# Two half transfers for every expert weight block in a two-layer hybrid trunk

## The chip, the cores and the metric

One core of one Trainium2 chip runs the whole program. The metric is the device time of one execution in microseconds (us), from the first to the last instruction and what lies around it; the median of the runs counts.

## What is computed

Two layers of an encoder trunk on 256 tokens of width 1024, all in fp32. Each layer has a token mixer and a channel mixer, both with norms and conditioning. The channel mixer of layer 0 is a dense SwiGLU; that of layer 1 sends each token to 2 of 8 experts. The change touches the experts alone:

```python
def swiglu(u, wg, wu, wd):
    return (jax.nn.silu(u @ wg) * (u @ wu)) @ wd

def moe_swiglu(h, w_router, b_router, w_gate_e, w_up_e, w_down_e):
    ...
    logits = (t @ w_router).astype(jnp.float32) + b_router.astype(jnp.float32)
    top_val, top_idx = lax.top_k(logits, TOP_K)
    gates = jax.nn.softmax(top_val, axis=-1)
    ...
    def expert_block(args):
        xblk, e = args
        return swiglu(xblk, w_gate_e[e], w_up_e[e], w_down_e[e])
    yb = lax.map(expert_block, (xb, blk_e)).reshape(p, d)
    y = jnp.zeros((n, d), h.dtype).at[tok_sorted].add(yb[dest] * g_sorted[:, None].astype(h.dtype))
```

The hidden width of an expert is 3584, so gate, up and down of one expert hold 3 x 14 = 42 MiB in fp32, and the eight experts 336 MiB. The other weights (about 120 blocks of up to 1 MiB) come before them through half of the same buffers.

## The kernel before

Each engine runs a program of its own, written out by hand; semaphores tie them together.

**Blocks and slots.** The weights of an expert are cut into 14 stages of 256 hidden columns. A stage has one block for gate and one for up (`[128, 8, 256]`: for each of 8 slices k of the input, 256 columns) and one for down (`[128, 2, 1024]`: for each of 2 halves f of the hidden columns, 1024 outputs). Each block is 1 MiB, 8 KB in each of 128 partitions, and lies in memory as 128 rows of 8 KB. Blocks are used in the order gate, up, then the down block of the stage before (`expert_uses`, lines 112 to 119). They go round 14 slots (`ring_e`, line 405): seven are the ring of the earlier weights (`ring` in the views), seven lie in the `arena`. In an expert 42 blocks go through, three rounds of the slots.

**SP** issues the transfers. `expert_use(i, e)` (lines 646 to 650) issues block i of expert e, which raises the semaphore `landed_e` of its slot by 16. Ahead of it SP waits until TensorE has done with the block that was in the slot (`last_use`, line 652: `gu_full` for gate and up, `down_done` for down). Three blocks of expert 0 are issued early; the loop from line 664 does all others, each one 14 blocks ahead of its use.

**TensorE** loops over the experts from line 1125. It reads the expert's number of tokens and branches to one of six versions of the code (`variants`, lines 545 to 554), for 32, 64, 128, 160, 192 or 256 tokens, each a tile of up to 128 tokens, or two. A version gathers the expert's tokens (lines 1140 to 1153), and then goes through the tiles of the 14 stages: `gate_up` of tile i, `turn` (a transpose of the activations) of tile i - 1, `down` of tile i - 2 (lines 1207 to 1217). Lines 1220 to 1228 spread the result back over the tokens. With fewer than 128 tokens in a tile `gate_up` uses line 1176: for each k, all of gate's and up's products, side by side in the array. With 128 it uses line 1182: all k for gate, then all k for up. `down` is line 1203, f outermost.

The waits for the weights are in `weights` (lines 1159 to 1162): `gate_up` waits for both blocks before its first product, `down` for its block before it waits for the activations (`at_ready`):

```python
def weights(kind, s):
    i = expert_at[kind, s]
    pe.wait_ge(landed_e[i % SLOTS_E], e * (16 * USES // SLOTS_E) + 16 * (i // SLOTS_E + 1))
    return ring_e[i % SLOTS_E]
```

**ScalarE and VectorE** take the gate products through silu and multiply with up (`act_ready`), and copy what `turn` made (`at_ready`). They don't look at `landed_e`.

In this input the experts run one behind the other as follows (widths of the version; times are from the views): experts 0 and 1 with 32, expert 2 with 128, expert 3 with 64, expert 4 with 160 (tiles of 128 and 32), expert 5 with 32, expert 6 with 192 (tiles of 128 and 64), expert 7 with 64.

Of the kernel before, what the change touches and what calls it, by code (L numbers as in the profile page):

```python
# [27 lines left out]
KD = D // P  # L28
# [13 lines left out]
SLOTS, SW = 7, 256  # L42
# [3 lines left out]
USES = 3 * STAGES  # L46
# [3 lines left out]
SLOTS_E = 2 * SLOTS  # L50
# [190 lines left out]
def build(nc, ap, out):  # L241
# [4 lines left out]
    expert_at = {u: i for i, u in enumerate(expert_list)}  # L246
# [8 lines left out]
    with ExitStack() as ctx:  # L255
# [6 lines left out]
        def sem(name):  # L262
            return ctx.enter_context(nc.semaphore(name))
# [69 lines left out]
        def cut(user, *dims):  # L333

            n = int(np.prod(dims))
            a = arena[:, top[user]:top[user] + n]
            top[user] += n
            return shaped(a, *dims)
# [66 lines left out]
        ring_e = [ring[:, (n_before + i) % SLOTS, :, :] for i in range(SLOTS)] + [cut("ffn", KD, SW) for _ in range(SLOTS_E - SLOTS)]  # L405
# [40 lines left out]
        wl_in = sem("wl_in")  # L446

        landed = [sem(f"landed{i}") for i in range(SLOTS)]
        landed_e = [sem(f"landed_e{i}") for i in range(SLOTS_E)]
        out_read = sem("out_read")  # L450
        const_set = sem("const_set")
        pj_full = sem("pj_full")
# [69 lines left out]
        def dense_use(kind, s):  # L522
            return 3 * s + KINDS.index(kind)
# [36 lines left out]
        def gate_up_of(m, u):  # L560

            w = SW if m > 32 else P
            if m == P:
                return PG[:, u % 2, 0:w], PG[:, u % 2, w:2 * w], slice(0, P), w
            return PG[0:P // 2, u % 2, 0:w], PG[P // 2:P, u % 2, 0:w], slice(P // 2, P), w
# [13 lines left out]
        def outputs(j, m):  # L581

            if m == P:
                return [(Y[:, 2 * j + h, :], h * 512, 512) for h in range(2)]
            n = P // m
            w = D // n
            return [(Y[i * m:(i + 1) * m, 2 * j + 2 * i // n, 0:w], i * w, w) for i in range(n)]

        def at_unit(e, n, u):


            return e * FT + (FT + (u + 1) * (2 // len(blocks(n))))

        def at_own(e, n, u):

            return e * FT + (u + 1) * (2 // len(blocks(n)))
# [21 lines left out]
        @block.sync  # L618
        def _(sp):
            def last_reader(kind, a, b):  # L620

                if kind == "ada":
                    return tr_full, TR.full(("ada", a, b // 4))
                if kind == "in":
                    return pj_full, PJ.full((IN_ITEM[b], a))
                if kind == "out":
                    return (y_full, 2 + a) if b == D // SW - 1 else (out_read, (D // SW - 1) * a + b + 1)
                return split_lo, dense_use(kind, b) + 1

            at = 0  # L630
            for u, (kind, a, b) in enumerate(uses):
                if u >= SLOTS:
                    sp.wait_ge(*last_reader(*uses[u - SLOTS]))
                n = KD * (b[1] if kind == "in" else SW)
                slot = ring[:, slot_of[u], :, :]
                if n < KD * SW:
                    slot = slot[:, :, 0:n // KD]
                else:
                    slot = slot.rearrange("p k c -> p (k c)")
                src = ap["weights"][0:1, at:at + P * n].rearrange("o (p c) -> p (o c)", p=P)  # L640
                if n < KD * SW:
                    src = src.rearrange("p (k c) -> p k c", k=KD)
                at += P * n
                sp.dma_start(slot, src).then_inc(landed[slot_of[u]], 16)

            def expert_use(i, e):

                slot = ring_e[i % SLOTS_E].rearrange("p k c -> p (k c)")
                src = ap["experts"][bass.ds(e * (USES * P) + i * P, P), :]
                sp.dma_start(slot, src).then_inc(landed_e[i % SLOTS_E], 16)  # L650

            def last_use(i, e):


                kind, s = expert_list[(i - SLOTS_E) % USES]
                return down_done if kind == "down" else gu_full, e * FT + ((FT if i >= SLOTS_E else 0) + 2 * s + 2)


            for i in range(EARLY):
                sp.wait_ge(*last_reader(*uses[n_before - SLOTS + i]))  # L660
                expert_use(i, 0)
            sp.wait_ge(y_full, 3)

            with sp.Fori(0, NE - 1) as e:
                for i in range(EARLY, USES):
                    sp.wait_ge(*last_use(i, e))
                    expert_use(i, e)
                for i in range(EARLY):
                    sp.wait_ge(*last_use(i, e + 1))
                    expert_use(i, e + 1)  # L670
            for i in range(EARLY, USES):
                sp.wait_ge(*last_use(i, NE - 1))
                expert_use(i, NE - 1)
            for b in range(TB):
                sp.wait_ge(out_ready, 2 * (b + 1))
                sp.dma_start(out[0][b * P:(b + 1) * P, :], tok[:, b, :]).then_inc(out_done, 16)
            sp.wait_ge(out_done, 16 * TB)
# [5 lines left out]
        def _(pe):  # L683
# [441 lines left out]
            with pe.Fori(0, NE) as e:  # L1125
                n_tok = pe.value_load(cnt[0:1, bass.ds(e, 1)], min_val=0, max_val=T)

                def expert(n):
# [11 lines left out]
                    for i in range(4):  # L1140
                        bank = take()
                        for j in range(2):
                            k = 2 * i + j
# [13 lines left out]
                    step = 2 // len(blocks(n))  # L1157

                    def weights(kind, s):
                        i = expert_at[kind, s]  # L1160
                        pe.wait_ge(landed_e[i % SLOTS_E], e * (16 * USES // SLOTS_E) + 16 * (i // SLOTS_E + 1))
                        return ring_e[i % SLOTS_E]

                    def gate_up(u, s, j, m):

                        w = [weights("gate", s), weights("up", s)]
                        if u >= 2:
                            pe.wait_ge(act_ready, at_unit(e, n, u - 2))
                        bank = PG[:, u % 2, :]
                        x = mixT[:, :, j * P:j * P + m]  # L1170
                        if m < P:
                            width = gate_up_of(m, u)[3]
                            for k in range(KD):
                                for i in range(P // m):
                                    c = i * width
                                    last = mm(bank[i * m:(i + 1) * m, 0:width], x[:, k, :],  # L1176
                                              w[c // SW][:, k, c % SW:c % SW + width],
                                              start=(k == 0), stop=(k == KD - 1))
                        else:
                            for i in range(2):  # L1180
                                for k in range(KD):
                                    last = mm(bank[:, i * SW:(i + 1) * SW], x[:, k, :], w[i][:, k, :],  # L1182
                                              start=(k == 0), stop=(k == KD - 1))
                        last.then_inc(gu_full, step)
# [12 lines left out]
                    def down(u, s, j, m):  # L1197

                        w = weights("down", s).rearrange("p k c -> p (k c)").rearrange("p (f c) -> p f c", f=2)
                        pe.wait_ge(at_ready, at_own(e, n, u))  # L1200
                        for f in range(2):
                            for o, c, width in outputs(j, m):
                                last = mm(o, actT[:, u % 2, f, 0:m], w[:, f, c:c + width],  # L1203
                                          start=(s == 0 and f == 0), stop=(s == STAGES - 1 and f == 1))
                        last.then_inc(down_done, step)

                    us = units(n)
                    for i in range(len(us) + 2):
                        if i < len(us):
                            gate_up(*us[i])  # L1210
                        if i == 0:
                            for b in range(2):
                                pe.wait_ge(ax_free[b], e * AX_F[b] + (AX_F[b] + 2))
                        if 1 <= i <= len(us):
                            turn(*us[i - 1])
                        if i >= 2:
                            down(*us[i - 2])

                    pe.wait_ge(ye_ready, e * 2 + 2)
                    for i in range(4):  # L1220
                        bank = take()
                        bl = blocks(n)
                        for q in range(2):
                            k = 2 * i + q
# [837 lines left out]
```

## Time and profile before

| what | value |
|---|---|
| median of 3 runs | 2094.73 us |
| lowest and highest of them | 2093.11 us and 7076.81 us |
| the profiled execution, its own time | 2095.57 us |
| its span, first to last instruction | 2093.8 us |
| TensorE's mean granted clock (1 is 2.4 GHz) | 0.883 |
| TensorE busy with products | 1811.4 us, 87% |
| weight queue q1 | 478.02 MB in 71616 packets |
| expert transfers | 336 of 1024.0 KB |

One of the three runs was far off; the other two lie within 2 us. In the views L1176 is line 1176 of the kernel, PE is TensorE's products and PEld its weight loads, "PEldq" and "SPq" are the sequencers of TensorE and SP, and q1 is SP's DMA queue; q8 and q14 carry the program's code. A DMA share of 1.00 means that the packets of all queues took the time of all sixteen DMA engines; a little over 1 is how packets are booked at a window's edges. In this table 1 MB is 10^6 bytes, and a block is 1.0486 MB.

### The profile page before, as it was taken

The numbers are of one execution on the slowest core, as the hardware profiler recorded it, in microseconds if no ns is written. First come the engines' busy times: TensorE is split into PE (matmuls) and PEld (weight loads), VectorE is DVE, ScalarE is ACT, GpSimd is POOL, SyncE is SP. The second block draws the span as 40 slices with busy tenths as digits, with TensorE's granted clock in tenths as the row PEclk, the third lists the DMA queues.
The fourth block names the chain that finished last, engine by engine and source line by source line (L and its number), as shares of the span: only waits on it lengthen the run. The fifth ranks groups of instructions, "written<-read, shape, count | busy, mean of one in ns | idle before, by whom it ended". The sixth has DMA issues, their size and how long they took to land.

```text
span 2093.8 us, 32178 instructions
## 1 busy us (share of the span) xinstructions
PE 1811.4 (87%) x13586; PEld 1349.1 (64%) x13587; DVE 443.5 (21%) x971; ACT 299.3 (14%) x585; POOL 43.1 (2%) x48
## 2 busy tenths in 40 slices
PE   3998979999899897665679979699997689999796
PEld 2776759999776676554467755477665466666453
DVE  1152235555415222111010011110011010000112
ACT  1222133333212211101000000100000010000101
POOL 0010000000001001000000000000000000000000
PEclk7997689999998767878789989799997889999797
DMA  6732357555342135599977759946463974444393
GB/s 235 286 121 80 149 188 286 183 183 189 131 147 110 75 155 223 240 419 402 420 316 288 297 205 417 388 164 240 196 241 159 420 318 181 181 181 181 112 418 139
DMA packets 75639, 484.86 MB, mean 232 GB/s; under 512 B 11872, under 2 KB 16236, under 8 KB 17516
## 3 DMA queue, kind: packets, MB, share of 16 engines
q1 hardware_dynamic: 71616, 478.02, 57.5%
q10 hardware_dynamic: 3756, 3.39, 0.6%
q8 instruction: 155, 2.54, 0.5%
q14 instruction: 112, 0.92, 0.1%
HBM read 480.33 MB, written 1.05 MB: 230 GB/s over the span
## 4 chain that ended last, share of the span: by engine, by line
PE 82%; issue 7%; DMA 5%; DVE 3%; ACTq 1%; ACT 1%; POOL 1%; SPq 0%; DVEq 0%; POOLq 0%
PE PG L1182 14%; PE Y L1203 13%; PE PG L1176 11%; DMA arena<-in_experts 5%; PE Y L796 4%; PE TRB L1193 3%; PE Y L804 3%; PE TRB L736 3%; PE Y L1049 3%; PE PG L760 3%; PE PG L762 3%; PE PG L761 3%; PE PG L1226 2%; PE TRB L1146 1%; PE TRB L1226 1%
## 5 line engine op out<-in xcount | busy, mean ns | idle before, releaser
L1960 DVE COPY arena<-TRB 128x64 f32<-128x64 f32 (+2 forms) x140 | 42.6, 305 | 835.4 <-PE TRB L1193 835.4
L1253 ACT ACTIVATE arena<-PG 128x256 f32<-128x256 f32 (+2 forms) x168 | 57.8, 344 | 1019.8 <-PE PG L1176 513.8
L1176 PE MATMUL PG<-ring,mixT 128*32 128x128 f32 (+1 forms) x2640 | 159.8, 320 | 28.2 <-issue 26.5
L1176 PE MATMUL PG<-arena,mixT 128*32 128x128 f32 (+1 forms) x2288 | 146.2, 336 | 36.3 <-issue 36.3
L1203 PE MATMUL Y<-arena 128*32 128x256 f32 (+2 forms) x896 | 171.6, 489 | 3.4 <-issue 3.4
L1176 PEld LDWEIGHTS PG<-ring,mixT 128*32 128x32 f32 (+1 forms) x2640 | 119.3, 124 | 75.3 <-issue 51.3
L1182 PE MATMUL PG<-ring,mixT 128*128 128x256 f32 x720 | 160.7, 381 | 1.3 <-DVE mixT L1943 1.3
L1176 PEld LDWEIGHTS PG<-arena,mixT 128*32 128x32 f32 (+1 forms) x2288 | 108.6, 131 | 78.5 <-issue 58.5
L1182 PEld LDWEIGHTS PG<-ring,mixT 128*128 128x128 f32 x720 | 135.4, 190 | 29.3 <-issue 11.9
L1182 PE MATMUL PG<-arena,mixT 128*128 128x256 f32 x624 | 139.9, 380 | 0.0
L760 PE MATMUL PG<-h_parts,parts 128*128 128x256 f32 x448 | 126.8, 283 | 10.0 <-DVE parts L1854 10.0
L1182 PEld LDWEIGHTS PG<-arena,mixT 128*128 128x128 f32 x624 | 117.0, 189 | 26.5 <-issue 10.2
L1203 PE MATMUL Y<-ring,arena 128*32 128x256 f32 (+2 forms) x672 | 127.9, 482 | 1.9 <-issue 1.9
L762 PE MATMUL PG<-h_parts,parts 128*128 128x256 f32 x448 | 126.8, 283 | 0.0
L761 PE MATMUL PG<-h_parts,parts 128*128 128x256 f32 x448 | 125.6, 280 | 0.0
L1146 PE MATMUL TRB<-arena,tok 128*128 128x128 f32 (+2 forms) x128 | 32.3, 446 | 89.3 <-issue 89.3
L1203 PEld LDWEIGHTS Y<-arena 128*32 128x32 f32 (+2 forms) x896 | 60.8, 134 | 71.5 <-issue 58.5
L1854 DVE TENSOR_TENSOR parts<-ring,parts 128x2048 fp32r<-128x2048 f32 x42 | 95.9, 2292 | 25.7 <-ACT parts L1253 25.7
L796 PE MATMUL Y<-hT,ring 128*128 128x256 f32 x416 | 95.3, 390 | 0.0
L760 PEld LDWEIGHTS PG<-h_parts,parts 128*128 128x128 f32 x448 | 85.4, 191 | 10.8 <-DVE parts L1854 10.4
L1146 PEld LDWEIGHTS TRB<-arena,tok 128*128 128x128 f32 x128 | 30.0, 330 | 94.0 <-issue 94.0
L1193 PEld LDWEIGHTS TRB<-con,arena 128*128 128x128 f32 (+1 forms) x448 | 62.8, 191 | 42.5 <-issue 40.5
(295 smaller groups left out, 2230.4 us busy)
## 6 DMA issues: line engine op xcount, KB each, us to landing
ring<-in_experts SPq DMA_DIRECT2D x168, 1024.0 KB, 9.1
arena<-in_experts SPq DMA_DIRECT2D x168, 1024.0 KB, 15.5
ring<-in_weights SPq DMA_DIRECT2D x116, 1024.0 KB, 6.3
ring<-in_weights SPq DMA_DIRECT2D x4, 512.0 KB, 4.0
tok<-in_x ACTq DMA_DIRECT2D x1, 1024.0 KB, 13.7
result<-tok SPq DMA_DIRECT2D x2, 512.0 KB, 2.8
ring<-in_weights SPq DMA_DIRECT2D x2, 432.0 KB, 6.2
arena<-in_w_ukv ACTq DMA_DIRECT2D x2, 384.0 KB, 4.2
```

Source lines behind the costliest of these rows:

```text
L736: last = mm(bank[32 * c:32 * c + 32, 0:SW], ccol[:, k, :], ring[:, slot_of[u], k, :], start=(k == 0), stop=(k == KD - 1))
L760: mm(out_, w_hi[w][:, c], x[0], start=first, stop=False, skip_group_check=True)
L761: mm(out_, w_hi[w][:, c], x[1], start=False, stop=False, skip_group_check=True)
L762: return mm(out_, w_lo[w][:, c], x[0], start=False, stop=last, skip_group_check=True)
L796: last = mm(bank_part, ring[:, s, k, c:c + m], hT[:, k, :], start=(k == 0), stop=(k == KD - 1))
L1146: last = mm(bank[:, j * T:j * T + w], tok[:, b, k * P:(k + 1) * P], oh[:, b, 0:w], start=(b == 0), stop=(b == TB - 1))
L1176: last = mm(bank[i * m:(i + 1) * m, 0:width], x[:, k, :], w[c // SW][:, k, c % SW:c % SW + width], start=(k == 0), stop=(k == KD - 1))
L1182: last = mm(bank[:, i * SW:(i + 1) * SW], x[:, k, :], w[i][:, k, :], start=(k == 0), stop=(k == KD - 1))
L1193: last = mm(tr[u % 2][:, f * P:(f + 1) * P], actK[r, u % 2, f * P:(f + 1) * P], ident[r, :], start=True, stop=True)
L1203: last = mm(o, actT[:, u % 2, f, 0:m], w[:, f, c:c + width], start=(s == 0 and f == 0), stop=(s == STAGES - 1 and f == 1))
L1226: last = mm(bank[:, q * T:(q + 1) * T], yeK[0:m, j, k * P:(k + 1) * P], gPT[0:m, j, :], start=(j == 0), stop=(j == len(bl) - 1))
L1854: V.tensor_tensor(w_lo[d % SPLITS], ring[:, slot_of[slot_of_dense(d)], :, :].rearrange("p k c -> p (k c)"), w_hi[d % SPLITS].bitcast(F32), ...
```

## The change

Each slot has two semaphores, `landed_e[slot][0]` and `[1]`. `expert_use` issues two transfers of `[128, 1024]`: the first 4 KB of each partition (slices k = 0 to 3 of gate and up, f = 0 of down), and the second 4 KB. Both are behind the one wait for the slot. On TensorE `weights` no longer waits. `half_landed(kind, s, q)` waits for half q of a block; `gate_up` calls it at k = 0 and k = 4, in a tile narrower than 128 for gate and up together, in a tile of 128 for the one in hand; `down` calls it ahead of each f. Nothing is computed differently.

```diff
-        landed_e = [sem(f"landed_e{i}") for i in range(SLOTS_E)]
+        landed_e = [[sem(f"landed_e{i}_{q}") for q in range(2)] for i in range(SLOTS_E)]
...
                 slot = ring_e[i % SLOTS_E].rearrange("p k c -> p (k c)")
                 src = ap["experts"][bass.ds(e * (USES * P) + i * P, P), :]
-                sp.dma_start(slot, src).then_inc(landed_e[i % SLOTS_E], 16)
+                for q in range(2):
+                    o = slice(q * KD * SW // 2, (q + 1) * KD * SW // 2)
+                    sp.dma_start(slot[:, o], src[:, o]).then_inc(landed_e[i % SLOTS_E][q], 16)
...
                     def weights(kind, s):
+                        return ring_e[expert_at[kind, s] % SLOTS_E]
+
+                    def half_landed(kind, s, q):
                         i = expert_at[kind, s]
-                        pe.wait_ge(landed_e[i % SLOTS_E], e * (16 * USES // SLOTS_E) + 16 * (i // SLOTS_E + 1))
-                        return ring_e[i % SLOTS_E]
+                        pe.wait_ge(landed_e[i % SLOTS_E][q], e * (16 * USES // SLOTS_E) + 16 * (i // SLOTS_E + 1))
...
                             for k in range(KD):
+                                if k % (KD // 2) == 0:
+                                    half_landed("gate", s, k // (KD // 2))
+                                    half_landed("up", s, k // (KD // 2))
                                 for i in range(P // m):
...
                                 for k in range(KD):
+                                    if k % (KD // 2) == 0:
+                                        half_landed(("gate", "up")[i], s, k // (KD // 2))
                                     last = mm(bank[:, i * SW:(i + 1) * SW], x[:, k, :], w[i][:, k, :],
                                               start=(k == 0), stop=(k == KD - 1))
...
                         for f in range(2):
+                            half_landed("down", s, f)
                             for o, c, width in outputs(j, m):
```

On TensorE, this is `gate_up`, `turn` and `down` of one tile of 128 tokens, in the version for two tiles, first before, then after the change. `landed_e2` and `landed_e3` are the semaphores of the slots of gate and up, `landed_e4` that of down; a second number is the half.

```order
L1182 MATMUL PG<-ring,mixT 128x256 [waits act_ready,landed_e3,landed_e2]
L1182 MATMUL PG<-ring,mixT 128x256 x15
L1188 REGISTER_ALU
L1193 MATMUL TRB<-con,arena 128x128 [waits act_ready]
L1193 MATMUL TRB<-con,arena 128x128
L1200 REGISTER_ALU [waits landed_e4]
L1203 MATMUL Y<-ring,arena 128x512 [waits at_ready]
L1203 MATMUL Y<-ring,arena 128x512 x3
```

```order
L1191 MATMUL PG<-ring,mixT 128x256 [waits landed_e2_0,act_ready]
L1191 MATMUL PG<-ring,mixT 128x256 x3
L1191 MATMUL PG<-ring,mixT 128x256 [waits landed_e2_1]
L1191 MATMUL PG<-ring,mixT 128x256 x3
L1191 MATMUL PG<-ring,mixT 128x256 [waits landed_e3_0]
L1191 MATMUL PG<-ring,mixT 128x256 x3
L1191 MATMUL PG<-ring,mixT 128x256 [waits landed_e3_1]
L1191 MATMUL PG<-ring,mixT 128x256 x3
L1197 REGISTER_ALU
L1202 MATMUL TRB<-con,arena 128x128 [waits act_ready]
L1202 MATMUL TRB<-con,arena 128x128
L1209 REGISTER_ALU
L1213 MATMUL Y<-ring,arena 128x512 [waits landed_e4_0,at_ready]
L1213 MATMUL Y<-ring,arena 128x512
L1213 MATMUL Y<-ring,arena 128x512 [waits landed_e4_1]
L1213 MATMUL Y<-ring,arena 128x512
```

No product has moved; the one wait point for the blocks of gate and up has become four, and the one of down two, inside the rows of products.

On SP, this is the issue of three blocks inside the loop over the experts, first before, then after.

```order
L650 ISA [waits down_done]
L650 DMA arena<-in_experts 128x2048
L666 REGISTER_ALU
L650 ISA [waits gu_full]
L650 DMA arena<-in_experts 128x2048
L650 ISA [waits gu_full]
L650 DMA arena<-in_experts 128x2048
```

```order
L668 REGISTER_ALU
L652 ISA [waits gu_full]
L652 DMA ring<-in_experts 128x1024
L652 ISA
L652 DMA ring<-in_experts 128x1024
L652 ISA [waits gu_full]
L652 DMA ring<-in_experts 128x1024
L652 ISA
L652 DMA ring<-in_experts 128x1024
L652 ISA [waits down_done]
L652 DMA arena<-in_experts 128x1024
L652 ISA
```

Each wait for a slot now stands ahead of two transfers instead of one; the order of the blocks is the same.

## Rows read from the trace of the kernel before

**Rows 1.** The page, part 4: the chain that ended last, by engine.

```profile
PE 82%; issue 7%; DMA 5%; DVE 3%; ACTq 1%; ACT 1%; POOL 1%; SPq 0%; DVEq 0%; POOLq 0%
```

**Rows 2.** Stretches of the expert phase: experts 0-1; 5; 2; 3; 4; 7.

```profile
core 0: us, PE busy (x) PEld busy (x) DVE busy (x) ACT busy (x) POOL busy (x), PEclk, DMA share, GB/s
858.80:1036.60 177.80, 114.96 (x2158) 86.73 (x2149) 19.40 (x66) 12.45 (x35) 0.00 (x0) 0.82 1.00 411
1602.60:1670.90 68.30, 45.26 (x964) 33.71 (x956) 6.52 (x25) 4.69 (x14) 0.00 (x0) 0.90 0.99 410
...
1061.00:1222.00 161.00, 158.85 (x650) 119.17 (x649) 13.84 (x36) 8.31 (x19) 0.00 (x0) 0.97 0.75 293
...
1239.00:1331.00 92.00, 90.75 (x653) 53.76 (x654) 12.85 (x36) 7.96 (x19) 0.00 (x0) 0.97 0.88 363
...
1352.00:1575.00 223.00, 220.88 (x1816) 155.16 (x1816) 24.07 (x68) 12.95 (x36) 0.00 (x0) 0.97 0.54 210
...
1975.00:2066.00 91.00, 89.75 (x653) 52.67 (x653) 12.85 (x36) 7.96 (x19) 0.00 (x0) 0.98 0.79 324
```

**Rows 3.** TensorE's waits (total us, times, longest), 858 to 1037; then 1036 to 2070.

```profile
PE PG L1176 <- issue: 41.5, 18, 4.1
...
PE PG L1176 <- issue: 23.9, 10, 4.1
```

**Rows 4.** TensorE in order of time (start, us), two stages and the last of expert 1.

```profile
999.50 3.64 PE L1176 MATMUL PG<-arena,mixT 128*32 128x128 f32 x64 [4.07 <-issue]
...
1006.95 1.96 PE L1176 MATMUL PG<-arena,mixT 128*32 128x128 f32 x64 [1.47 <-issue]
...
1036.72 3.65 PE L1176 MATMUL PG<-arena,mixT 128*32 128x128 f32 x64 [2.57 <-issue]
```

**Rows 5.** DMA, 980 to 1030 us: queue, kind: packets, MB, share; issues and us to landing.

```profile
q1 hardware_dynamic: 2869, 20.90, 100.5%
...
ring<-in_experts SPq DMA_DIRECT2D x12, 1024.0 KB, 25.8
```

**Rows 6.** TensorE's branches (ns min/median/max, first and last start): four under load, two quiet.

```profile
L1125 PEldq COMPARE_BRANCH  x1: 6055/6055/6055, 1046.3 to 1046.3; - x1
...
L551 PEldq COMPARE_BRANCH  x1: 5925/5925/5925, 1222.2 to 1222.2; - x1
...
L1125 PEldq COMPARE_BRANCH  x1: 7177/7177/7177, 1336.6 to 1336.6; - x1
...
L551 PEldq COMPARE_BRANCH  x3: 70/80/6456, 1686.4 to 1686.6; - x3
...
L553 PEldq COMPARE_BRANCH  x1: 3344/3344/3344, 1956.0 to 1956.0; - x1
...
L551 PEldq COMPARE_BRANCH  x3: 82/3894/4897, 1965.1 to 1969.2; - x3
```

**Rows 7.** DMA, 2089 to 2093.8 us: the two result transfers, pieces of 4 KB.

```profile
q1 hardware_dynamic: 288, 1.05, 54.6%
```

**Rows 8.** DMA, 126 to 130.5 us: one weight transfer of 512 KB, pieces of 512 bytes.

```profile
q1 hardware_dynamic: 1040, 0.52, 38.6%
```

**Rows 9.** The chain in order of time (start, us), two stages of expert 3.

```profile
1259.65 3.47 PE PG L1176 x32
...
1265.62 3.47 PE PG L1176 x32
```

**Rows 10.** TensorE's sequencer at the wait for weights (ns min/median/max).

```profile
L1161 PEldq EVENT_SEMAPHORE  x24: 51/51/51, 856.5 to 1982.1; - x24
```

**Rows 11.** TensorE in order of time (start, us), a stage of expert 2.

```profile
1102.35 3.60 PE L1203 MATMUL Y<-arena 128*128 128x512 f32 x8
1105.79 1.46 PE L1182 MATMUL PG<-arena,mixT 128*128 128x256 f32 x6
```

**Rows 12.** SP's transfers to the arena and all landings (min/median/max), 1100 to 1210 us.

```profile
L650 SPq DMA_DIRECT2D arena<-in_experts x16: 332/333/333, 1106.1 to 1204.5; - x16
...
DMA to landing us min/median/max: 4.7/6.7/9.6
```

## The prediction

> **What bounds the kernel now.** I read four things in this order. First the chain that ended last [rows 1]: TensorE carries 82% of it, "issue" 7% and DMA 5%. So the whole is a TensorE kernel, and a change to weight transfers can only act where the chain leaves TensorE.
>
> Then the table of stretches [rows 2]. The experts run from about 858 to 2066 us, and there are two kinds. In the first stretch (experts 0 and 1, few tokens) and the second one (expert 5) the DMA engines are busy at a share of 1.00 and 0.99 while TensorE is busy for 115.0 of 177.8 us and 45.3 of 68.3 us: these wait for weights. In the other four TensorE is busy for over 98% of the time and the DMA share is 0.54 to 0.88 (expert 6, not shown, is like expert 4): there the ring of 14 blocks is full or filling. The waits of L1176 with "issue" as their cause are 41.5 us over 18 times up to 1037 us and 23.9 us over 10 times behind it [rows 3]. Here "issue" is the wait for `landed_e`, which the view doesn't name.
>
> Third, the pace inside a starved expert [rows 4]. The products of two successive stages begin at 999.50 and 1006.95 us: 7.45 us for three blocks, 2.48 us a block. In the window 980 to 1030 us the weight queue's packets take 100.5% of the sixteen engines, and a transfer lands 25.8 us after its issue [rows 5], some ten blocks of 2.48 us: about ten transfers are queued. So the queue is never empty there, and what sets the time is engine time per block, not the wait of one product.
>
> Fourth, what TensorE does between experts. The branches into the next expert's code take from 5.93 to 7.18 us while weights are moving, and 3.34 to 4.90 us while the queue is quiet [rows 6].
>
> **The price of a block in two halves.** A whole block is 128 pieces of 8 KB and 16 semaphore writes, 144 packets; the halves make 256 pieces of 4 KB and 32 writes, 288 packets. In rows 5 the queue moves 20.90 MB (19.93 blocks) in 1.005 x 16 x 50 = 804 us of engine time, 40.3 us a block, or 2.52 us on each of 16 engines. The two result transfers are exactly the new shape, 256 pieces of 4 KB with 32 small ones, though they write to HBM: 0.546 x 16 x 4.8 = 41.9 us [rows 7], 2.62 us a block, 0.10 more. The weight transfer with pieces of 512 bytes took 0.386 x 16 x 4.5 = 27.8 us for half a block [rows 8], 3.47 us a block with 2080 packets. By these two shapes a packet costs (55.6 - 40.3) / (2080 - 144) = 8 ns, and 144 packets more cost 1.14 us of engine time, 0.07 us a block. The bounds of a loss are thus 0.07 near by and 0.95 (the 512-byte row) far off; a gain is excluded, since no byte goes away. I take 0.08, between the two near rows.
>
> It counts only where DMA decides. By rate times time of rows 2, 411 GB/s over 177.8 us is 70 blocks, and 410 GB/s over 68.3 us is 27. So +5.6 us for experts 0 and 1, and +2.2 us for expert 5.
>
> Experts 3 and 7 could become starved, since a stage takes 5.97 us (1259.65 to 1265.62) [rows 9] and eats three blocks, of which DMA brings 5.97 / 2.48 = 2.4 now and 5.97 / 2.56 = 2.33 later. Over 14 stages that draws 8.4 blocks now and 9.4 later from a stock of 14. They stay TensorE's: nothing.
>
> **What earlier halves give.** In a starved expert each stage may begin when the first half of `up` is there, 1.28 us sooner. That makes TensorE early, but the last half still comes at DMA's pace and the ring still has ten transfers queued, so the next stage is not sooner by it. It counts once where DMA's chain hands over to TensorE: the last stage of expert 1 (3.65 us of products from 1036.72 [rows 4], of which the first half now lies before the second half's landing) and the same place in expert 5. Each gains at most a half's time, 1.28 us, since half of 3.65 is more than that; for both I take -2.6 us. At the far end, the release of a slot to SP comes with the last product as before and gives nothing.
>
> **The added waits.** The two waits for gate and up of a tile become four (one more place in a tile narrower than 128, three more at 128), and the one for down becomes two. They stand in the row of products, so all of TensorE's later products queue behind them, and ScalarE and VectorE behind those. Where the half has landed they are only sequencer work: 51 ns for a semaphore instruction [rows 10]. The L1182 group at 1105.79 follows the down products of 1102.35 + 3.60 = 1105.95 without a gap, though three waits stand before it, as the order above shows [rows 11]. So at 128 tokens they cost nothing, hidden by products of 0.2 us. The narrowest tiles issue fastest; in expert 4 there are 14 of them. Two more semaphore instructions and a register one, at most 0.14 us each, make 0 to 1.9 us; I take 1.0. In starved experts the wait for DMA covers them. If the cover were gone there too (42 tiles), it would be 6 us.
>
> **SP.** Twice the issues: 0.33 us each [rows 12] with 0.1 us of registers, under 0.9 us a block against 2.56. If ten transfers is what the queue holds, ten halves are 12.8 us of work queued instead of 25; a lone transfer needs 4.7 us from issue to landing [rows 12], so the queue still doesn't run dry.
>
> **Code loading.** TensorE's branch instructions wait for code that comes over the same 16 engines. Under load eight of them lie on the chain (two between experts 1 and 2, one behind expert 2, three behind 3, two behind 5), mean 6.45 us; the seven quiet ones have 4.14 [rows 6]; of the eight the first, both extremes and the last are shown, of the seven the extremes. The excess of 2.3 us is time behind queued weights. What of it goes with halves isn't shown by any row: between 0 (if the loader waits behind bytes) and all of it. An engine's share of one transfer is 2.5 us now, close to the excess, and 1.28 us then. I take it that the loader waits for about a transfer's share, and that the excess halves: 8 x 1.15 = -9.2 us. Between experts 0 and 1 it gives nothing, for DMA is the chain there.
>
> The Trainium skill (DMA: Bandwidth & Descriptors, Queues, rings and completion order) says that an engine takes turns between its queues at whole packets of some 9 to 17 descriptors, and one transfer here is nine to each engine. By that rule the sum would be the one I take; by turns at every 8 KB piece, 0.31 us now (2.52 / 8) and half later, it would be -1 us for this term. The trace's excess of 2.3 us is far above one piece, so it leans to the rule.
>
> **Sum.** +5.6 + 2.2 - 2.6 + 1.0 - 9.2 = -3.0 us, on the profiled execution's 2095.57 us: 2092.6. The median of the runs, 2094.73, lies 0.8 us below that execution, so 2092 for the median.
>
> **Rivals.** *Loader unmoved*: branches stay at 6.45 us under load, and what is left is the packet price at experts 0, 1 and 5: +6.2 us, 2101, slower than before. For it: the 16 KB code packets themselves can't be split by the change, and engines may queue by bytes. Against: the excess is so near to one transfer's share. It decides as soon as less than 6.2 / 8 = 0.8 us goes from each branch.
>
> *The waits shrink*: each of the 28 waits of rows 3 becomes 1.28 us shorter: -36 us, 2059. Against it are the DMA share of 1.00 and the strict 7.45 us.
>
> *Half blocks move slowly*: a 4 KB piece of an 8 KB row is read worse than the result's own, up to the 512-byte price: 97 blocks x 0.95 = +92 us, and experts 3 and 7, then starved (5.97 / 3.47 = 1.7 blocks a stage, 18 of a stock of 14), some 10 us more: 2200. It passes 2% from 2.95 us a block on. Against: both near rows. The Trainium skill (DMA: Bandwidth & Descriptors, Rules for kernel authors) wants at least 1 MiB per transfer; its fixed cost of about 2 us per transfer, if paid in turn, would go this way. Rows 5 bear it out only as latency: with ten queued, 2.5 us is all that a block takes.
>
> *The change does nothing that shows*: both terms small, 2095.
>
> **Chances.** Forecast 0.47, loader unmoved 0.36, waits shrink 0.05, slow halves 0.05, nothing 0.07. The low end is the whole excess gone (-18.4) with free waits: 2095.57 - 0.8 + 5.6 + 2.2 - 2.6 - 18.4 = 2082, say 2083. The high end is the loader unmoved, with 0.10 a block (+2), waits at 1.9 (+0.9) and no gain at the hand-over (+2.6): 2107. A measurement of this kernel tells about 2% (42 us) from no change. Beyond it on the fast side only a far stronger form of the shrinking waits lies, 0.01; on the slow side most of slow halves, 0.04; within, 0.95.
>
> **What would show it.** Right: in a starved stretch the queue's share stays at 1.00 and the stage takes 3 x 2.56 = 7.7 us; stages of experts 2, 3, 4, 6 and 7 keep their times; branches under load fall to about 5.3 us; transfers land some 13 us after their issue. Loaded branches above 6.2 us would make the forecast wrong in favour of the first rival, a share below 0.95 or a stage above 8.3 us in favour of slow halves, and a stage below 7.3 us in favour of shrinking waits.

## The result, and the profile after

The changed kernel took 2101.92 us (median of 10 runs, 2099.15 to 2107.13), the kernel before beside it 2097.2 us (median of 10). The ratio of the means, without the one far-off run of the kernel before, is 1.0031, 95% interval 1.0019 to 1.0044: about 6.5 us slower (4.7 us by the medians). A second set, shown below, gave 1.0045 (1.0027 to 1.0062). Both are inside the stated range, but the forecast had the sign wrong; what came is nearest to the rival that was called *loader unmoved*, with its 2101 us.

The profiled execution took 2100.6 us, its span 2098.8 us. The page's chain and weight queue, to be held against [rows 1]:

```profile
q1 hardware_dynamic: 120000, 478.04, 60.3%
...
PE 75%; SPq 8%; issue 7%; DMA 4%; DVE 3%; ACT 1%; ACTq 1%; POOL 1%; DVEq 0%; POOLq 0%
```

The same bytes move in 120000 packets instead of 71616, which is 336 x 144 more, and take 60.3% of the engines' time. "SPq 8%" is new in the chain. I don't read it as a cost by itself: an issue takes up to 2.9 us in the starved stretch and 0.33 us where the queue has room, so SP is held back while the queue is full. The chain is followed through SP there instead of through the transfers and TensorE, whose share falls from 82% to 75%. The DMA engines have a share of 1.01 in the same stretch, so they never wait for SP. A DMA-bound stretch is booked in another place.

The stretches that answer to those of [rows 2] (experts 0-1; 5; 2; 3; 4; 7):

```profile
core 0: us, PE busy (x) PEld busy (x) DVE busy (x) ACT busy (x) POOL busy (x), PEclk, DMA share, GB/s
860.00:1043.20 183.20, 116.59 (x2169) 87.14 (x2158) 19.40 (x66) 12.55 (x35) 0.00 (x0) 0.80 1.01 397
1606.00:1675.40 69.40, 47.93 (x904) 34.67 (x904) 6.41 (x25) 3.21 (x12) 0.00 (x0) 0.83 1.02 401
1064.00:1225.00 161.00, 158.17 (x650) 118.74 (x650) 13.62 (x36) 8.93 (x20) 0.00 (x0) 0.98 0.84 302
1243.00:1337.00 94.00, 90.96 (x651) 54.14 (x652) 12.84 (x36) 7.95 (x19) 0.00 (x0) 0.97 0.89 345
1357.00:1578.00 221.00, 217.71 (x1816) 153.59 (x1816) 24.05 (x68) 12.92 (x36) 0.00 (x0) 0.99 0.61 218
1980.00:2072.00 92.00, 89.83 (x653) 52.84 (x653) 12.84 (x36) 7.95 (x19) 0.00 (x0) 0.99 0.82 321
```

The first two rows are starved as before, with a full DMA share, but the rate has gone from 411 to 397 GB/s and from 410 to 401 GB/s.

TensorE in order of time (start, us) in two starved stages of expert 1, and the last one; this answers to [rows 4]:

```profile
1027.92 3.64 PE L1183 MATMUL PG<-ring,mixT 128*32 128x128 f32 x64 [2.73 <-DMA ring<-in_experts]
...
1035.60 1.08 PE L1183 MATMUL PG<-arena,mixT 128*32 128x128 f32 x32 [1.57 <-DMA arena<-in_experts]
1036.88 1.08 PE L1183 MATMUL PG<-arena,mixT 128*32 128x128 f32 x32 [0.19 <-DMA arena<-in_experts]
...
1043.28 3.21 PE L1183 MATMUL PG<-arena,mixT 128*32 128x128 f32 x64 [3.91 <-DMA arena<-in_experts]
```

Two things can be read here. The stages come 7.68 us apart instead of 7.45. And the halves do what they are for: at 1035.60 TensorE works on the first half, waits, and begins the second at 1036.88, 1.28 us later, as the second half lands. At 1027.92, with the products slower than the transfer, there is no gap. TensorE is early in every stage, and the next stage is not a bit sooner for it.

DMA from 980 to 1030 us, for [rows 5]:

```profile
q1 hardware_dynamic: 5583, 20.33, 101.9%
...
ring<-in_experts SPq DMA_DIRECT2D x15, 512.0 KB, 15.9
```

A half lands 15.9 us after its issue; at 1.28 us each about twelve are queued.

TensorE's branches (ns, min/median/max), for [rows 6], four under load and two quiet:

```profile
L1127 PEldq COMPARE_BRANCH  x1: 6052/6052/6052, 1051.7 to 1051.7; - x1
...
L551 PEldq COMPARE_BRANCH  x1: 6934/6934/6934, 1225.3 to 1225.3; - x1
...
L1127 PEldq COMPARE_BRANCH  x1: 7312/7312/7312, 1343.0 to 1343.0; - x1
...
L551 PEldq COMPARE_BRANCH  x1: 6556/6556/6556, 1691.0 to 1691.0; - x1
...
L553 PEldq COMPARE_BRANCH  x1: 3677/3677/3677, 1960.4 to 1960.4; - x1
...
L551 PEldq COMPARE_BRANCH  x3: 82/4359/4591, 1970.0 to 1974.5; - x3
```

Nothing fell. The eight loaded branches on the chain have a mean of 6.53 us, before 6.45. The spread between executions is as large: in the traces of the experiments below the same eight have 6.42 us in the repeat of the change and 6.43 us in the first experiment, which also has halves, against 6.48 and 6.43 us in the two kernels with whole blocks and ten queued.

The last two stages of expert 3, which the prediction had left out of the sum:

```profile
1312.09 3.62 PE L1183 MATMUL PG<-ring,mixT 128*64 128x256 f32 x32
...
1318.05 3.64 PE L1183 MATMUL PG<-arena,mixT 128*64 128x256 f32 x32
...
1325.49 3.69 PE L1183 MATMUL PG<-arena,mixT 128*64 128x256 f32 x32 [1.30 <-DMA arena<-in_experts]
```

The last gap is 7.44 us, of which 1.30 us are a wait for DMA. A stage of expert 3 took 5.97 us [rows 9], and in the trace of before the last ones are as long:

```profile
1307.23 3.62 PE L1176 MATMUL PG<-ring,mixT 128*64 128x256 f32 x32
...
1313.19 3.64 PE L1176 MATMUL PG<-arena,mixT 128*64 128x256 f32 x32
...
1319.16 3.64 PE L1176 MATMUL PG<-arena,mixT 128*64 128x256 f32 x32
```

The last of these stages was already close to its block there. SP issued the `up` block of stage 13 in the kernel before as follows, and it landed 17.2 us later, at 1318.8 us, 0.4 us ahead of its first use at 1319.16:

```profile
L650 SPq DMA_DIRECT2D arena<-in_experts x1: 333/333/333, 1301.6 to 1301.6; - x1
...
DMA to landing us min/median/max: 17.2/17.2/17.2
```

In expert 7 it landed at 2053.0 us and was used from 2053.94.

### The profile page after: what moved, and what is told of

Its sections match the earlier page's. It is cut to its first block, busy times and chain, and to the rows that moved or that the text cites. A ratio compares the mean times of both kernels' runs of the same rounds, so it can differ in the third digit from the quotient of the medians.

```text
span 2098.8 us, 33330 instructions
## 1 busy us (share of the span) xinstructions
PE 1809.9 (86%) x13586; PEld 1347.0 (64%) x13587; DVE 443.4 (21%) x971; ACT 299.0 (14%) x585; POOL 43.0 (2%) x48
## 3 DMA queue, kind: packets, MB, share of 16 engines
q1 hardware_dynamic: 120000, 478.04, 60.3%
## 4 chain that ended last, share of the span: by engine, by line
PE 75%; SPq 8%; issue 7%; DMA 4%; DVE 3%; ACT 1%; ACTq 1%; POOL 1%; DVEq 0%; POOLq 0%
PE PG L1191 14%; PE Y L1213 11%; PE PG L1183 8%; SPq L652 8%; PE Y L798 4%; DMA arena<-in_experts 4%; PE Y L806 3%; PE TRB L1202 3%; PE Y L1051 3%; PE PG L762 3%; PE PG L764 3%; PE PG L763 3%; PE TRB L738 2%; PE PG L1236 2%; PE TRB L1148 1%
## 5 line engine op out<-in xcount | busy, mean ns | idle before, releaser
L1213 PEld LDWEIGHTS Y<-arena 128*32 128x32 f32 (+2 forms) x896 | 60.3, 134 | 67.2 <-issue 54.5
```

Of the source, the lines that this page charges most:

```text
L1213: last = mm(o, actT[:, u % 2, f, 0:m], w[:, f, c:c + width], start=(s == 0 and f == 0), stop=(s == STAGES - 1 and f == 1))
```

## The experiments

The theory after the result ("starved" is a stretch in which TensorE waits for blocks, the "hand-over" its end, where TensorE sets the pace again, and the "loader" whatever fetches TensorE's code): (a) a packet costs a fixed time, which counts in starved stretches; (b) experts 3 and 7 have become starved at their ends; (c) TensorE's hand-over from the last starved block gains once per starved expert chain; (d) met waits are free; (e) the loader's excess depends neither on pieces nor on the queue. All ratios are to the kernel before in the same set.

**Halves without the new waits.** Against the kernel before:

```diff
-                sp.dma_start(slot, src).then_inc(landed_e[i % SLOTS_E], 16)
+                for q in range(2):
+                    o = slice(q * KD * SW // 2, (q + 1) * KD * SW // 2)
+                    sp.dma_start(slot[:, o], src[:, o]).then_inc(landed_e[i % SLOTS_E], 16)
...
-  pe.wait_ge(landed_e[i % SLOTS_E], e * (16 * USES // SLOTS_E) + 16 * (i // SLOTS_E + 1))
+  pe.wait_ge(landed_e[i % SLOTS_E], e * (32 * USES // SLOTS_E) + 32 * (i // SLOTS_E + 1))
```

> Two transfers of 512 KB per block, both raising one semaphore by 16, and TensorE waits as in the kernel before, once for the whole block (32 per use). Theory (the price is engine time per block, 0.08 us, at about 97 starved blocks, and experts 3 and 7 turn starved at their end): without the hand-over gain the time is 2 to 5 us above the changed kernel, so +8 to +12 us against the kernel before; a starved stage takes 7.68 us. Rival (the added waits inside the products cost the time): this kernel has none of them and is within 2 us of the kernel before.

Measured: 1.0064 (1.0047 to 1.008), 2108.03 against 2094.36 us, +13.4 us by the ratio. The interval, +9.8 to +16.8 us, reaches into the theory's +8 to +12, and the loss is 1.4 to 2 times that of the full change (+9.4 and +6.5 us); the rival is out. TensorE at the end of expert 3:

```profile
1310.68 3.62 PE L1178 MATMUL PG<-ring,mixT 128*64 128x256 f32 x32
...
1317.32 3.69 PE L1178 MATMUL PG<-arena,mixT 128*64 128x256 f32 x32 [0.51 <-issue]
...
1324.99 3.69 PE L1178 MATMUL PG<-arena,mixT 128*64 128x256 f32 x32 [1.48 <-issue]
```

6.64 and 7.67 us instead of 5.97 and 5.97: 2.4 us lost by the starts of products, and as much in expert 7. The `up` block of stage 13 landed at 1324.9 us here, just before the 1324.99. With the waits per half the same place loses 1.5 us in expert 3 and 1.1 us in expert 7 (1.4 and 0.8 us in the repeat below), since the last stage may begin at the first half. From the same trace, the time from the first product of expert 0 to the last stage of expert 1 is 5.7 us longer than before, and that from expert 5's first product to its last stage 2.1 us.

**The new waits without the halves.** Against the changed kernel:

```diff
-                for q in range(2):
-                    o = slice(q * KD * SW // 2, (q + 1) * KD * SW // 2)
-                    sp.dma_start(slot[:, o], src[:, o]).then_inc(landed_e[i % SLOTS_E][q], 16)
+                sp.dma_start(slot, src).then_inc(landed_e[i % SLOTS_E][0], 16)
...
-                        pe.wait_ge(landed_e[i % SLOTS_E][q], e * (16 * USES // SLOTS_E) + 16 * (i // SLOTS_E + 1))
+                        pe.wait_ge(landed_e[i % SLOTS_E][0], e * (16 * USES // SLOTS_E) + 16 * (i // SLOTS_E + 1))
```

> One transfer of 1 MB per block as before, but TensorE waits at all the places of the changed kernel, for the same semaphore each time. Theory: met waits are hidden, 0 to +2 us against the kernel before, and the first products of up in the 128-wide tiles may start before up has landed, which gives nothing. Rival (waits carry the loss): +5 to +7 us, and stages of experts 2, 4 and 6 get longer by 0.1 us or more each.

Measured: 0.9994 (0.9985 to 1.0002), at most +0.4 us. No cost of the waits shows. In expert 4, the one with the narrow tiles that the prediction gave 1.0 us, TensorE reads

```profile
1392.93 1.96 PE L1181 MATMUL PG<-ring,mixT 128*32 128x128 f32 x64
...
1407.64 0.62 PE L1181 MATMUL PG<-arena,mixT 128*32 128x128 f32 x13
```

and a stage is 14.71 us, as from 1394.93 to 1409.64 us in the kernel before. Even mid-row waits at a product spacing of 0.03 us (64 products in 1.96 us) are hidden.

**Pieces of 4 KB in one transfer.** Source and destination written as three dimensions:

```diff
-  sp.dma_start(slot, src).then_inc(landed_e[i % SLOTS_E], 16)
+  sp.dma_start(slot.rearrange("p (h c) -> p h c", h=2),
+               src.rearrange("p (h c) -> p h c", h=2)).then_inc(landed_e[i % SLOTS_E], 16)
```

> One transfer per block, one semaphore, waits as before, but source and destination are written as 128 x 2 x 1024, so that a block should move in 256 pieces of 4 KB with 16 semaphore writes. Theory (a fixed 8 to 9 ns per packet): 128 packets more a block instead of 144, so nine tenths of e1's loss, +7 to +10 us, starved stage 7.66 us. Rival (the second transfer costs, by its issue or its semaphore writes): within 2 us of the kernel before. If the pieces stay 8 KB nothing changes and the run only repeats the kernel before.

Measured: 0.9994 (0.9984 to 1.0004). It tells nothing of pieces: the page has 71616 packets on q1 as before, so the two dimensions were joined again. It is a repeat of the kernel before, and shows that this comparison is good to 0.1%. So it doesn't tell whether the smaller pieces or the second transfer and its semaphore writes cost; the packets' own records do, under the next run.

**Quarters.** As the first experiment with four transfers and 64 per block.

> Four transfers of 256 KB per block (pieces of 2 KB) on one semaphore, waits as in the kernel before. Theory (a fixed 8 to 9 ns per packet): 576 packets a block instead of 144, three times the added packets of e1, 0.24 us a block: starved stage 8.2 us, and three times e1's loss, about +39 us. Rival (a fixed price per transfer, or none below some size): twice e1's loss or less, +27 us at most. The branches under load: about 6.5 us again if the loader doesn't wait behind a transfer's share, near 5 us if it does.

Measured: 1.0205 (1.0191 to 1.022), +43 us, 3.2 times the +13.4 us of halves. A starved stage:

```profile
1031.72 3.64 PE L1178 MATMUL PG<-ring,mixT 128*32 128x128 f32 x64 [3.06 <-issue]
...
1039.86 2.86 PE L1178 MATMUL PG<-ring,mixT 128*32 128x128 f32 x64 [2.15 <-issue]
```

8.14 us. Single stages scatter, so I take several of expert 1 for the price: 7.44 us a stage in the kernel before (five stages, 999.50 to 1036.72), 7.66 us in the first experiment (five, 1004.06 to 1042.34) and 8.11 us here (four, 1015.52 to 1047.94). For each added packet that is 0.21 / 3 x 16 / 144 = 7.8 ns with halves and 0.66 / 3 x 16 / 432 = 8.1 ns with quarters: about 8 ns, and straight.

Halves and quarters add transfers in the same proportion as packets (one and three a block), so these times alone would fit a price per transfer as well. The packets' own records decide. From 970 to 1030 us a piece of 8 KB is booked at 314 ns on average, one of 4 KB at 165 ns and one of 2 KB at 88 ns, so two pieces take 11 to 16 ns more than one of twice the size; a semaphore write is booked at 9 ns, and the 16 added with halves are 0.15 us of the 1.2 us of engine time that a block in halves costs. The share of the engines stays above 1.00, so nothing is lost between transfers. It is 1.005, 1.019 and 1.046 for whole blocks, halves and quarters from 980 to 1030 us, more than packets at a window's edges explain: booked times overlap a little, so the price of 8 ns is taken from the stages and not from the records.

The eight loaded branches have a mean of 6.2 us, 96% of the 6.45 us before. But they didn't all stay. The first ones behind experts 1, 3 and 5 took 5.03, 4.69 and 5.24 us instead of 6.05, 6.10 and 6.28; the other five took 6.5 to 7.4 us, 0.35 us more than before on average. What makes the first ones shorter is open.

**A queue of three, and of two.** Whole blocks; SP waits for the landing of an earlier block (its loop over the experts written out, so that waits are on constants):

```diff
+                o = i - 3
+                if o >= 0:
+                    sp.wait_ge(landed_e[o % SLOTS_E], e * (16 * USES // SLOTS_E) + 16 * (o // SLOTS_E + 1))
...
-            with sp.Fori(0, NE - 1) as e:
+            for e in range(NE - 1):
```

> Whole blocks, but SP issues block i only when block i - 3 has landed, so that three transfers are queued at most instead of ten (the loop over the experts is written out on SP so that waits are on constants). Theory A (the loader's excess under load of 2.3 us does not depend on what is queued): branches stay at 6.5 us, the stage at 7.45 us, and the time within -2 to +3 us of the kernel before. Theory B (the loader waits behind queued bytes): branches fall to 5.5 us or less and the time by 6 to 15 us.

> As e6_queue_of_three with two transfers at most. A lone transfer takes 4.7 us to land, of which 2.3 us are not its own bytes, so two queued ones just don't cover it on every engine: starved stages of 7.5 to 8.5 us, the time +5 to +40 us. Theory A: branches under load still 6 to 6.5 us; theory B: 5 us or less, since engines run dry between blocks.

Measured: three 0.9998 (0.9984 to 1.0013), two 1.0158 (1.0131 to 1.0185), +33 us. With three queued a transfer lands 7.4 us after its issue instead of 25.8 [rows 5], and the branches stay:

```profile
ring<-in_experts SPq DMA_DIRECT2D x10, 1024.0 KB, 7.4
...
L1131 PEldq COMPARE_BRANCH  x1: 5752/5752/5752, 1051.9 to 1051.9; - x1
...
L551 PEldq COMPARE_BRANCH  x1: 6036/6036/6036, 1224.0 to 1224.0; - x1
...
L1131 PEldq COMPARE_BRANCH  x1: 7117/7117/7117, 1338.7 to 1338.7; - x1
...
L551 PEldq COMPARE_BRANCH  x3: 70/80/6296, 1691.6 to 1691.9; - x3
```

Mean of the eight: 6.46 us. Theory B is out: whether three transfers are queued or ten doesn't matter to the loader. With two queued, when the share of the DMA engines falls to 0.95, the first branches behind experts 1, 2, 3 and 5 take 4.7, 3.7, 4.3 and 4.6 us, and the second at each of these places still takes 6 us and more.

The pace with three queued isn't quite that of ten in the profiled execution, which at 2101.44 us was the slowest of its twelve: from 980 to 1030 us it moved 406 GB/s against 420, and seven stages of expert 1 came 7.7 us apart on average, not the expected 7.45. The time of all twelve shows no loss.

**Halves for the last blocks alone.** Against the changed kernel; with it TensorE waits on the second semaphore for these blocks only:

```diff
+                if i < USES - 4:
+                    sp.dma_start(slot, src).then_inc(landed_e[i % SLOTS_E][0], 16)
+                    return
                 for q in range(2):
```

> Only the last four blocks of every expert (gate and up of stage 13, the last two downs) are fetched in halves with a wait for each half; the other 38 are whole as before. Theory (halves gain once where the DMA chain hands over to TensorE, 1.28 us at experts 1 and 5 and at the last stage of 3 and 7, and cost 0.08 us a block): -1 to -4 us against the kernel before. Rival (early halves never reach the end, because the next thing is late anyway): 0 to +1 us.

Measured: 0.9976 (0.9964 to 0.9988), -5 us, beyond the expected -1 to -4. A later set of the same kernel, and two relatives, were to show whether that holds:

> The same kernel as e5_last_blocks_halved, since quarters gave no gain where halves had given 5 us. Theory (hand-over gain real): -3 to -6 us again. Rival (chance between sets of runs): 0 to -2 us.

> Halves, with a wait each, only for gate and up of stage 13 of every expert; both last downs and all other blocks whole. Theory (the gain at the hand-over is the last up block's first half, 1.28 us at four experts): the same as e5_last_blocks_halved had, -3 to -6 us. Rival (that gain was in the last down blocks, or e5's -5 us was chance): 0 to -2 us.

> As e5_last_blocks_halved, but the last four blocks of every expert come as four transfers each and gate_up of every tile waits at k = 0, 2, 4, 6. Theory (a hand-over gains the share of the block that is worked on before its end lands): up to 0.6 us more at each of four hand-overs than with halves, less 0.16 us a block for these blocks: -4 to -8 us against the kernel before. Rival (halves had already used all that the hand-over gives): the same as with halves, -5 us, or a loss by waits.

Measured: the same kernel again 0.9991 (0.9982 to 1.0), only gate and up of stage 13 0.9991 (0.9982 to 1.0), quarters 0.9995 (0.9986 to 1.0004). So -5 us was in part chance between sets: the same kernel gave -1.9 us, with an interval that touches no change, and a gain of some 2 us is all that I claim. It also fits the traces better: in the kernel before only experts 1 and 5 hand over from a starved chain, 2 x 1.28 us at most, and experts 3 and 7 don't wait at all. My expectation of four hand-overs was wrong. Quarters miss their expectation of -4 us for the same reason, and pay more packets. The hand-over itself can be seen in the first of these kernels:

```profile
1023.14 3.27 PE L1189 MATMUL PG<-ring,mixT 128*32 128x128 f32 x64 [2.45 <-DMA ring<-in_experts]
...
1030.61 1.96 PE L1189 MATMUL PG<-arena,mixT 128*32 128x128 f32 x64 [2.79 <-DMA arena<-in_experts]
...
1036.92 3.21 PE L1189 MATMUL PG<-arena,mixT 128*32 128x128 f32 x64 [2.94 <-DMA arena<-in_experts]
```

7.47 us between whole blocks, and 6.31 us to the stage whose blocks come in halves: 1.2 us sooner.

**The change again, and the change without experts 3 and 7.** The second has whole blocks there; SP raises the second semaphore itself.

```diff
+                if e in (3, 7):
+                    sp.dma_start(slot, src).then_inc(landed_e[i % SLOTS_E][0], 16)
+                    sp.sem_inc(landed_e[i % SLOTS_E][1], 16)
+                    return
                 for q in range(2):
```

> The changed kernel itself, to stand beside the others of this set: +4 to +8 us against the kernel before.

> The changed kernel, but experts 3 and 7 get whole blocks (one transfer on the first semaphore; SP itself raises the second), SP's loop over the experts written out. Theory (of the changed kernel's loss, experts 3 and 7 turning starved at their ends make up about 2.7 us each, less the hand-over gain of 1.3 us each): 3 to 5 us faster than e11, and in experts 3 and 7 the last stages come 5.97 us and about 6.1 us apart. Rival (nothing is lost there, as the prediction had it): within 1 us of e11.

Measured: the change 1.0045 (1.0027 to 1.0062), +9.4 us, a little over the expected +8; without the two experts 1.0036 (1.0021 to 1.005). The difference of some 2 us has the expected sign and is smaller than the expected 3 to 5, but the intervals overlap, so the times alone don't show it. The trace does, for the place:

```profile
1310.29 3.62 PE L1187 MATMUL PG<-ring,mixT 128*64 128x256 f32 x32
...
1316.25 3.64 PE L1187 MATMUL PG<-arena,mixT 128*64 128x256 f32 x32
...
1322.22 2.99 PE L1187 MATMUL PG<-arena,mixT 128*64 128x256 f32 x26
```

The last two stages are 5.96 and 5.97 us apart by the starts of these groups, as in the kernel before. (The last group has fewer products only because the view ends there.) In expert 7 it is 5.96 and 5.98 us. Something else took part of this gain in the profiled execution: the first branch behind expert 1, on the chain, took 7.38 us, where the repeat of the change has 6.08.

```profile
L1131 PEldq COMPARE_BRANCH  x1: 7378/7378/7378, 1050.4 to 1050.4; - x1
```

## Why the prediction was wrong

The step that failed is the one on code loading: it gave -9.2 us for shorter branches, and the branches didn't get shorter. Step by step:

- **The price of a packet** was right: 0.08 us a block forecast, 0.07 us measured (7.66 against 7.44 us a stage over five stages; the two stages shown above give 0.077). Its use on experts 0, 1 and 5, +5.6 and +2.2 us, came out at 5.7 and 2.1 us in the kernel with halves and the old waits. The near rows, the two result transfers and the 512-byte pieces, carried this, and *slow halves* didn't happen: a 4 KB piece of an 8 KB row is booked at 165 ns, the whole row at 314.
- **Experts 3 and 7** were the first error. "They stay TensorE's: nothing" set 14 stages' average draw against the stock of 14. But the last stage's up block is needed when that stage begins, the first slot comes free only with the first product's end, a transfer lands 4.7 us after its issue [rows 12], and the first stages are shorter than 5.97 us. In the kernel before the last up block of expert 3 came in just as it was needed. 26 blocks go through by then, and 0.07 to 0.08 us on each is 2 us late against a margin of 0.4 us in expert 3 and 0.9 us in expert 7. Measured in the starts of the last stages: 2.4 us at each of the two with the old waits, 1.5 and 1.1 us with the halves' waits.
- **The hand-over** had the right mechanism and about the right size: 1.2 us where only the last blocks come in halves, and 0.9 and 1.3 us at experts 3 and 7 (2.4 less 1.5 and 1.1). In the changed kernel it happens four times, since 3 and 7 are starved too. The kernel with the old waits is slower than the change by 4 to 7 us (1.0064 against 1.0031 and 1.0045), which is about four times 1.28 us.
- **The added waits** cost nothing that shows (0.9985 to 1.0002, at most +0.4 us); 1.0 us had been put there.
- **Code loading** was the error that turned the sign. "I take it that the loader waits for about a transfer's share, and that the excess halves" had one thing for it, that 2.3 us is near 2.5 us. Branches took 6.45 us before, 6.53 us with halves (6.42 in the repeat), 6.46 us with three transfers queued instead of ten, and 6.2 us with quarters. The -9.2 us were nothing. Without them the forecast's own terms give +6.2 us. The turn-taking rule of the Trainium skill (DMA: Bandwidth & Descriptors, Queues, rings and completion order), to which this step leaned, is not borne out as an account of the excess: a half is again nine packets to each engine, of half the bytes, and the excess didn't halve. The other reading, of a piece at a time, would have taken 0.15 us from each branch; the three traces with halves (6.53, 6.42 and 6.43 us) show no such fall against the three with whole blocks (6.45, 6.48 and 6.43). What the loader waits for under load stays open.
- **SP** was as forecast in that no engine ran dry; the queue held about twelve halves, not ten, so that a half landed 15.9 us after its issue and not the forecast 13.

With the measured terms the sum is +5.7 + 2.1 + 2 x 2.4 for the packets, -4 x 1.28 for the hand-overs, which makes +7.5 us. The two measurements are +6.5 and +9.4 us. Without the hand-overs it is +12.6, and the kernel with halves and the old waits measured +13.4. That the rival's 2101 was met so closely is in part luck: it, too, had nothing for experts 3 and 7 and 1.0 us for waits that cost nothing. One small term stays outside the sum: the second branch behind expert 2 took 5.1 to 5.5 us in the three traces with halves and 4.6 to 4.8 us in the three with whole blocks.

The rule of the Trainium skill to fetch at least 1 MiB per transfer, cited beside *slow halves* (DMA: Bandwidth & Descriptors, Rules for kernel authors), is right here in its sign, but what half of that size costs is 3% of a block's time, not a second fixed cost. The cost of about 2 us per transfer that the prediction takes from the skill is fitted there (Anatomy of one DMA — SWDGE (gpsimd) path) to transfers that GpSimd issues; here SP issues them, and with ten queued no run shows it as time paid in turn.

## What to carry to other kernels

Where transfers are queued ten deep, a stage waits for the engines and not for its block: cutting the block lets its reader start early and makes every later block a little later, and the early start is paid out only once, at the last block before the reader becomes the bound again. To judge whether a nearly starved stretch stays fed, go by the last block's deadline against the first free slot plus the latency plus the blocks between, not by average rates and a full stock. And a duration that lies near another one is no mechanism: the -9.2 us hung on such a likeness, and had no row behind them.

## What was not expected of the hardware

- Each added DMA packet took about 8 ns of an engine's time, the same for pieces of 4 KB (7.8) and 2 KB (8.1).
- TensorE's branches into new code take about 6.5 us while the weight queue is busy and about 4.1 us while it is quiet, whether the queue has three or ten transfers and whether a piece is 8 or 4 KB. With pieces of 2 KB, or two transfers queued, the first branch behind an expert mostly took 3.7 to 5.3 us and the next 5.9 us or more; why is open.
- Three queued transfers of 1 MB give the time of ten (0.9998, 0.9984 to 1.0013), though the one profiled execution moved 406 instead of 420 GB/s; two don't (1.0158, a share of 0.95).
- Two access dimensions that lie one behind the other are joined: the packets stayed at 71616.
